# The start of a down-projection without a barrier, and its raw rows in seven slots

## The reference

```
g_pre, val = split(rmsnorm(x) @ w_ffn_up, 2)      # 1024 -> 2 x 2816
g          = causal_dwconv(g_pre, width 3)
x          = x + (gelu(g) * val) @ w_ffn_down     # 2816 -> 1024
y          = rmsnorm(x) * norm_final
```

## Time and profile before

| what | us |
|---|---|
| median of 3 runs | 3394.83 (3393.14 to 3395.13) |
| profiled execution, its own time | 3398.22 |
| its span | 3395.8 |
| first matmul of the down-projection at | 2817.30 |
| PE busy in the span | 3048.7 (90%) |
| ACT, DVE, POOL busy | 759.3, 1442.4, 1214.2 |

### The profile page before, as it was taken

The page is one execution under the profiler, slowest core; times in us unless marked ns, Lnnn a source line. Parts: engine busy times, 40 slices in busy tenths (PEclk is TensorE's granted clock), DMA queues, the critical chain, the costliest instruction groups (busy, mean ns, idle before and its releaser), DMA issues.

```text
span 3395.8 us, 47191 instructions
## 1 busy us (share of the span) xinstructions
PE 3048.7 (90%) x15400; PEld 2666.9 (79%) x15400; DVE 1442.4 (42%) x1910; ACT 759.3 (22%) x1530; POOL 1214.2 (36%) x574
## 2 busy tenths in 40 slices
PE   4898988956888888897899999999999997999998
PEld 4798978833444444446899999999999997899998
DVE  4212433348555555626215555544455542211221
ACT  5100332212232233334002000000000003443342
POOL 1011110144566666604765221222122213444443
PEclk8899999966899899998899999999999998999999
DMA  5311334355777776744344111111111104554553
GB/s 180 95 65 57 84 105 104 87 99 179 234 228 250 225 234 205 226 138 147 106 139 126 51 44 47 47 44 42 50 50 50 44 30 170 187 178 159 172 192 109
DMA packets 253579, 422.51 MB, mean 124 GB/s; under 512 B 49265, under 2 KB 156954, under 8 KB 248906
## 3 DMA queue, kind: packets, MB, share of 16 engines
q1 hardware_dynamic: 167986, 322.58, 30.5%
q10 hardware_dynamic: 85152, 97.07, 9.5%
q0 software_dynamic: 288, 1.05, 0.1%
HBM read 337.21 MB, written 83.46 MB: 124 GB/s over the span
## 4 chain that ended last, share of the span: by engine, by line
PE 67%; DMA 9%; POOL 8%; DVE 6%; issue 4%; SPq 3%; ACT 2%; POOLq 0%; ACTq 0%; DVEq 0%
PE PS L2413 33%; PE PS L2115 13%; PE PS L2499 4%; PE PS L2501 3%; PE PS L2500 3%; POOL prod L870 3%; DMA Kpg<-in_cache_k 3%; PE PS L2307 2%; DMA GR<-gT 2%; SPq L565 2%; PE PS L2404 1%; SPq L558 1%; POOL DL L990 1%; PE PS L2096 1%; DMA xin<-in_x_prompt 1%
## 5 line engine op out<-in xcount | busy, mean ns | idle before, releaser
L2413 PE MATMUL PS<-MH,VH 128*128 128x416 f32 x2000 | 708.3, 354 | 11.6 <-POOL VL L933 8.3
L2413 PE MATMUL PS<-ML,VH 128*128 128x416 f32 x2000 | 702.3, 351 | 0.0
L2413 PE MATMUL PS<-MH,VL 128*128 128x416 f32 x2000 | 701.9, 351 | 0.0
L2413 PEld LDWEIGHTS PS<-MH,VH 128*128 128x128 f32 x2000 | 376.1, 188 | 18.7 <-issue 13.3
L990 POOL TENSOR_TENSOR DL<-DR,DH 128x1408 fp32r<-128x1408 f32 x80 | 258.5, 3231 | 354.2 <-ACT DH L1410 354.0
L927 POOL TENSOR_TENSOR VR<-VR,gains 128x1024 f32<-128x1024 f32 x52 | 98.8, 1900 | 795.9 <-PE PS L2413 695.4
L2413 PEld LDWEIGHTS PS<-ML,VH 128*128 128x128 f32 x2000 | 377.2, 189 | 4.2 <-issue 0.8
L2413 PEld LDWEIGHTS PS<-MH,VL 128*128 128x128 f32 x2000 | 376.5, 188 | 4.8
L2499 PE MATMUL PS<-GH,DH 128*128 128x416 f32 x880 | 320.9, 365 | 46.7 <-POOL DL L990 28.3
L870 POOL TENSOR_TENSOR prod<-Kpg,qb 128x1024 f32<-128x1024 f32 x118 | 284.2, 2408 | 172.6 <-DMA Kpg<-in_cache_k 135.7
L2307 PE MATMUL PS<-PT,VA 128*65 128x416 f32 (+16 forms) x816 | 337.1, 498 | 4.5 <-ACT PT L1264 4.0
(11 more groups left out here) (274 smaller groups left out, 4604.9 us busy)
## 6 DMA issues: line engine op xcount, KB each, us to landing
Kpg<-in_cache_k SPq DMA_DIRECT2D x256, 256.0 KB, 4.3
Vpg<-in_cache_v SPq DMA_DIRECT2D x256, 256.0 KB, 4.2
DR<-in_w_down SPq DMA_DIRECT2D x80, 704.0 KB, 4.1
gT<-GO ACTq DMA_DIRECT2D x110, 208.0 KB, 1.9
GR<-gT SPq DMA_DIRECT2D x55, 416.0 KB, 4.9
VR<-in_w_up SPq DMA_DIRECT2D x44, 512.0 KB, 3.5
WR<-in_w_stream SPq DMA_DIRECT2D x21, 512.0 KB, 3.6
Qst<-qT SPq DMA_DIRECT2D x16, 520.0 KB
```

What stands on the lines that cost most here:

```text
L2413: mm = e.matmul(PS[:, j, 0:BW], w[:, u, k], x[:, k, cols(j)], start=(k == 0 and q == 0), stop=(k == KC - 1 and q == 2))
```

## The change

**The barrier goes.** Each engine has its own waits instead. The `m4` tiles are laid out so that some lie where the last up-chunk no longer reads: `GR` slots 0 to 2 and `DR[0]` over `VR` and the even weight slot of `VS` (which now holds `VH` and `VL`), free after chunk 50 (`u_mm >= 255`); `DH[0]` and `DL[0]` behind all the up-projection's tiles. `GH`, `GL`, the other four `GR` slots, `DR[1]` and the rest wait for the last up matmul (`u_mm >= 260`). `XS` moves to another stack.

**Work during the last up-chunk.** SP loads pairs 0 to 2 and `DR[0]`; POOL makes `DH[0]` (a copy of its own) and `DL[0]`.

**Seven raw slots** `GR` instead of three, so a `fetch_inner` waits for the pair seven before it. In block 0 it waits for the stores of its own rows too.

The core of the diff:

```diff
-            e.wait_ge(phase_end, 12)
+            e.wait_ge(v_lo, 52)
+            e.wait_ge(u_mm, 5 * 51)
...
             def fetch_inner(j, q):
                 f = FH * j + q
-                if f >= 3:
-                    e.wait_ge(gg_lo, f - 2)
-                e.dma_start(GR[:, f % 3], gT[...]).then_inc(gr_ld[f % 3], 16)
+                if j == 0:
+                    for st in go_st:
+                        e.wait_ge(st, 16 * NB * (q + 1) + 1)
+                if f >= NGR:
+                    e.wait_ge(gg_lo, f - NGR + 1)
+                e.dma_start(GR[f % NGR], gT[...]).then_inc(gr_ld[f % NGR], 16)
...
             fetch_down(0, 0, 0)
             for q in range(1, 3):
                 fetch_inner(0, q)
+            e.wait_ge(u_mm, 5 * 52)
+            fetch_inner(0, 3)
             fetch_down(1, 0, 1)
-            fetch_x2(0, 0, 0, 0)
-            e.dma_start(gfin[:], ...)
-            for q in range(3, FH):
+            for q in range(4, NGR):
                 fetch_inner(0, q)
...
+                if j == 0:
+                    fetch_down(2, 1, 0)
+                    fetch_inner(0, 7)
+                    fetch_x2(0, 0, 0, 0)
+                    fetch_inner(0, 8)
+                    fetch_down(3, 1, 1)
+                    for q in range(9, FH):
+                        fetch_inner(0, q)
+                    fetch_x2(1, 1, 0, 1)
+                    e.dma_start(gfin[:], ...)
...
# GpSimd
-            e.sem_inc(phase_end, 1)
-            e.wait_ge(phase_end, 12)
+            e.wait_ge(dr_ld[0], 16)
+            e.tensor_copy(DH[0][:], DR[:, 0]).then_inc(d_hi, 1)
+            low_down(0, 0)
+            low_down(1, 1)
...
# ScalarE
-            for s in go_st: ...
-            e.sem_inc(phase_end, 1)
-            e.wait_ge(phase_end, 12)
+            e.wait_ge(u_mm, 5 * 52)
...
-            split_down(0, 0)
             for q in range(3):
                 inner_high(0, q)
+            e.wait_ge(d_lo, 1)
             split_down(1, 1)
             for q in range(3, FH):
                 inner_high(0, q)
+                if q == 7:
+                    split_down(2, 0)
...
                 act_pair(0, first=True)
-                with e.Fori(1, 3) as i:
-                    act_pair(i)
-                act_pair(3, last=True)
+                act_pair(1)
+                act_pair(2, fills=FILLS[0])
+                act_pair(3, last=True, fills=FILLS[1])
# VectorE and TensorE: the barrier's two lines go; dve_pair as act_pair
```

More of the change, by code:

```diff
@@ L30 @@
 FH = FC // 2
+NGR = 7
 RING = 16
@@ L55, with inner_landed @@
 BIG = -1e30
+def inner_landed(f):
+    return 16 * (f // NGR) + 16 + (32 * 4 * NS if f % NGR >= 3 else 0)
 class Steps:
@@ L349, in build @@
         GL = sb("GL", [P, RING, 2, BW], F32R, m4)
[L350 to L353, removed]
         YX = sb("YX", [P, 2, BW], F32, m4)
-        YT = sb("YT", [P, 4, DM], F32, m4)
-        ysq = sb("ysq", [P, 4, P], F32, m4)
+        gfin = sb("gfin", [P, DM], F32, m4)
         yr = sb("yr", [P, 4], F32, m4)
         yq = sb("yq", [P, 4, KC], F32, m4)
-        gfin = sb("gfin", [P, DM], F32, m4)
+        ysq = sb("ysq", [P, 4, P], F32, m4)
+        GRb = sb("GRb", [P, NGR - 3, 2, BW], F32, m4)
+        under = sb("under", [P, 2 * KC * TP - 2 * RING * 2 * BW - 2 * BW - DM - 4 - 4 * KC - 4 * P - 2 * (NGR - 3) * BW],
+                   F32, m4)
+        GRa = sb("GRa", [P, 3, 2, BW], F32, m4)
+        DR = sb("DR", [P, 2, FH, P], F32, m4)
+        YT = sb("YT", [P, 4, DM], F32, m4)
+        DH1 = sb("DH1", [P, FH, P], F32R, m4)
+        DL1 = sb("DL1", [P, FH, P], F32R, m4)
+        over = sb("over", [P, 6 * KC * P + FC * 4 + FC * 2 * NS + TP + TP + 2 + TP + 2 + 4 * BW + 2 * P - 6 * BW - 2 * FH * P
+                           - 4 * DM - 2 * FH * P], F32, m4)
+        DH0 = sb("DH0", [P, FH, P], F32R, m4)
+        DL0 = sb("DL0", [P, FH, P], F32R, m4)
+        DH, DL = (DH0, DH1), (DL0, DL1)
+        GR = [GRa[:, n] for n in range(3)] + [GRb[:, n] for n in range(NGR - 3)]
         m4.close()
@@ L483, in build @@
         dk = sem("dk")
-        gr_ld = [sem(f"gr_ld{s}") for s in range(3)]
+        gr_ld = [sem(f"gr_ld{s}") for s in range(3)] + kg_ld
         gg_hi = sem("gg_hi")
@@ L766, in sync_pair @@
                             fetch_x2(8 * j + oc + 2, 0 if last else oc + 2, j + 1 if last else j, 0)
-                        if last and ahead:
+                        if j < NB - 1:
                             for q in fills[c]:
                                 fetch_inner(j + 1, q)
-                with e.Fori(0, 3) as i:
-                    sync_pair(i)
-                sync_pair(3, True)
+                if j == 0:
[7 more added lines that the diff above has]
+                    fetch_x2(1, 1, 0, 1)
+                    e.dma_start(gfin[:], a["norm_final"][0].partition_broadcast(P)).then_inc(nf_ld, 16)
+                    fetch_down(4, 2, 0)
+                    fetch_down(5, 2, 1)
+                    fetch_x2(2, 2, 0, 0)
+                    sync_pair(1)
+                else:
+                    with e.Fori(0, 2) as i:
+                        sync_pair(i)
+                sync_pair(2, False, FILLS[0])
+                sync_pair(3, True, FILLS[1])
         @block.gpsimd
@@ L982, in _, with low_down @@
             e.wait_ge(nlo, 15)
+            e.wait_ge(nst, 15)
+            e.wait_ge(nhi, 20)
             e.wait_ge(v_lo, 52)
-            e.sem_inc(phase_end, 1)
-            e.wait_ge(phase_end, 12)
-            with e.Fori(0, 8 * NB) as i:
+            def low_down(n, h):
+                e.wait_ge(d_hi, n + 1)
+                e.tensor_tensor(DL[h][:], DR[:, h], DH[h][:].bitcast(F32), ALU.subtract).then_inc(d_lo, 1)
+                e.wait_ge(d_lo, n + 1)
+            e.wait_ge(dr_ld[0], 16)
+            e.tensor_copy(DH[0][:], DR[:, 0]).then_inc(d_hi, 1)
+            low_down(0, 0)
+            low_down(1, 1)
+            with e.Fori(1, 8 * NB) as i:
                 for h in range(2):
-                    e.wait_ge(d_hi, 2 * i + h + 1)
-                    e.tensor_tensor(DL[:, h], DR[:, h], DH[:, h].bitcast(F32), ALU.subtract).then_inc(d_lo, 1)
-                    e.wait_ge(d_lo, 2 * i + h + 1)
+                    low_down(2 * i + h, h)
         @block.scalar
@@ L1456, in _, with act_pair @@
                 inner_high(0, q)
+                if q == 7:
+                    split_down(2, 0)
             for j in range(NB):
-                def act_pair(i, first=False, last=False):
+                def act_pair(i, first=False, last=False, fills=((), (), (), ())):
                     n, oc = 16 * j + 4 * i, 8 * j + 2 * i
-                    fills = {0: (0, 1, 2), 1: (3, 4), 2: (5, 6, 7, 8, 9), 3: (10,)}
                     for c in range(4):
-                        if not (j == NB - 1 and last and c == 3) and not (j == 0 and first and c == 0):
+                        if not (j == NB - 1 and last and c == 3) and not (j == 0 and first and c < 2):
                             split_down(n + c + 1, (c + 1) % 2)
@@ L1473, in act_pair @@
                             take_sum(oc, 2 * i, 0)
-                        if last and j < NB - 1:
+                        if j < NB - 1:
                             for q in fills[c]:
@@ L1485, in _ @@
             e.wait_ge(y_st, 64 * NB + 16)
+            for s in go_st:
+                e.wait_ge(s, 16 * NB * FC // 2 + 1)
+            for s in tt_st:
+                e.wait_ge(s, 16 * FC + 1)
+            e.wait_ge(f_st, 96)
         @block.vector
@@ L2061, in _, with dve_pair @@
                 inner_low(0, q)
-            e.wait_ge(nf_ld, 16)
             for j in range(NB):
-                def dve_pair(i, first=False, last=False):
+                def dve_pair(i, first=False, fills=((), (), (), ())):
                     oc = 8 * j + 2 * i
-                    fills = {0: (0, 1, 2), 1: (3, 4), 2: (5, 6, 7, 8, 9), 3: (10,)}
                     for c in range(4):
-                        if last and j < NB - 1:
+                        if j < NB - 1:
                             for q in fills[c]:
@@ L2078, in _ @@
                 dve_pair(0, first=True)
-                with e.Fori(1, 3) as i:
-                    dve_pair(i)
-                dve_pair(3, last=True)
+                dve_pair(1)
+                dve_pair(2, fills=FILLS[0])
+                dve_pair(3, fills=FILLS[1])
             final_apply(NB - 1)
```

41 lines of the change are left out of this document (14 added, 27 removed).

## The result

The changed kernel takes 3353.92 us in the median of 4 runs (3347.84 to 3359.2), the kernel before 3394.98 (3393.14 to 3402.36): a ratio of 0.9871, 95% interval 0.9854 to 0.9888. The profiled execution took 3355.78 us, its span 3353.6. The prediction was 3353.

A forecast was written before the change was run, and what follows sets the result against it. TensorE was taken to bound the kernel by standing still or running slowly at the barrier, the first rows and block ends; -10.3 + 0.5 - 6.7 - 25, taken as -42, gave 3353 us, range 3343 to 3371.

The forecast's parts named there:

- The first idle time: At the barrier before the down-projection: PE's idle time falls from 14.53 to 4.2 us, -10.3 us.
- POOL under the last up-chunk: Last up-chunk: POOL's copy and subtraction hold DVE up to 6.4 us; 0.5 us reaches the end, bounds 0 and 3.1.
- The first rows: First three halves of the down-projection: 26 us from PE's start against 32.7 before, -6.7 us.
- The 1 us for slow matmuls: First three halves: allowance for slow matmuls after idle times, 1.6 to 2.8 us each, part hidden under row waits.
- The block ends: Ends of blocks 0 to 3: of 28.1 us lost there 3 stay, -25 us.
- What stays: Each later block's first pair: a store wait holds ACT 3.41 us, untouched by the change; seven chunks take 92.2, not 90.1.
- The sum: Whole kernel: -10.3 + 0.5 - 6.7 - 25 = -41.5 us, taken as -42.
- Block ends giving half back: Ends of blocks: rows land later and stalls drag slow matmuls, 4 x 4 us more, -29, 3366 us; chance 0.20.
- waits only exchanged at the start: First three halves: third half ends as late after PE's start, POOL's `DL` blocking DVE's lows; near 3361 us; chance 0.09.
- Slower by row copies ahead of weight copies: Row copies ahead of weight copies in six halves a block, not four, make ACT late; 3402 us; chance 0.03.

The follow-up runs named there:

- the repetition: The changed kernel run once more, unaltered, on the chip of two other follow-up kernels: 3357.03 us, ratio 0.9858 to the kernel before.
- the swap: Changed kernel with y-store issues and first `take_sum` behind weight copies, new start order, and row loads ahead of `fetch_x2`: 3346.71 us, ratio 0.983.
- the spreading alone: Changed kernel with three raw row slots in place of seven, the spread placing of row loads kept: 3364.3 us, ratio 0.9904.

## Why the prediction was right, step by step

- **The first idle time.** Forecast 4.2 us, measured 4.25, ended by `GL` on DVE. The term of -10.3 is right for the kernel as it stands; the experiments divide X in other parts, since a barrier also delays what is issued behind it.
- **POOL under the last up-chunk.** Its copy took 1.36 us, bounded at 3.2, its subtraction 3.23. DVE's op beside the subtraction took 3.50 us, where the same line takes 0.65 elsewhere. In all DVE is busy for 18.03 us in the last up-chunk and was for 14.84: 3.2 us more, not 6.4. All of it is absorbed, since DVE waits as long for PE ahead of its last multiply as before, 3.30 us against 3.29. So 0 reached the end and not 0.5. The Trainium skill's rule (SBUF — State Buffer, Who interferes with whom) holds as to the blocking; the 3.1 us at the end that the prediction worked out with it did not appear. POOL, then DVE:

```profile
2787.61 1.36 POOL L1029 CAST DH<-DR 128x1408 fp32r<-128x1408 f32 x1 [22.14 <-DMA DR<-in_w_down]
2789.05 3.23 POOL L1025 TENSOR_TENSOR DL<-DR,DH 128x1408 fp32r<-128x1408 f32 x1
```

```profile
2789.23 3.50 DVE L2029 SCALAR_TENSOR_TENSOR GC<-GP,ftab,GC 128x416 f32<-128x416 f32 x1
...
2805.15 0.59 DVE L2052 TENSOR_TENSOR GO<-GC,R 128x416 f32<-128x416 f32 x1 [3.30 <-PE PS L2452]
```

- **The first rows.** 26 us forecast from PE's start to the third half's end, 25.3 measured in the first profile and 27.1 in the repetition. Both waits foreseen came, for pair 3 and pair 8, and they ended 6.7 and 15.5 us after PE's start, where 7.2 and 15.7 were forecast. The size of the first was not worked out right: by the prediction's own times PE would have waited 3.8 us for pair 3, not "about 2", and it waited 1.53, since slow matmuls had filled the time (5.2 us for three pairs instead of 3.4). The second came as 2.83, 2.9 by its times. The 1 us for slow matmuls was a guess between two outcomes, 0 and 1.6 us behind pair 8, and the two profiles show one each.
- **The block ends.** 3 us forecast to stay, 1.8 measured, where it was expected: at half 17, not at half 16. That the loads behind `fetch_x2` are the cause is shown by the swap, which takes it to 0 in its one profile. What the prediction gave to "seven slots" and to "three row copies instead of five" in one breath, the experiments separate: for the ends the spreading alone is enough.
- **What stays.** The chunk of 14.87 us stayed in all four blocks, but its cause was misread. I took a wait with a name for the cause and did not look at what stood ahead of the late weight copy in ACT's queue. It changed no term of the sum.
- **The sum.** -42 forecast; -42.2 between the two spans. That they agree to 0.2 us is in part luck: +2.2 come from the phases ahead of the change, -1.6 from one slow chunk before, and X moves by 1.8 from profile to profile.
- **Rivals.** Block ends giving half back, and waits only exchanged at the start: neither came. Slower by row copies ahead of weight copies: pair 2 shows no wait. The undisturbed chunks take 12.92 us, where before they were 12.84 and 12.92 by turns, about 1 us in all; its cause stays open.

## What to carry to other kernels

In hand-ordered queues a late instruction is late for what stands in front of it, so look at the queue up to it, not at the wait that the view names. Spreading prefetches until few stand ahead of an urgent copy can be worth as much as deeper buffers, and where it is, the buffers' gain lies elsewhere, here at the cold start. A barrier costs more than the idle time behind it: everything issued behind it is late too, and loads moved ahead of it recover only a part.

## What the runs showed of the hardware

- A DVE op with two SBUF operands begun during a GpSimd subtraction ended only behind it, by 0.4 to 0.9 us: 3.50 instead of 0.65 us, and 3.41 and 3.33 instead of 1.03.
- Behind one and the same wait (2.83 and 2.84 us) PE ran on at the higher level in one profile and fell to the lower for ten matmuls in another: 1.6 us. The estimate of this start cannot be closer than that.
- One program's phases ahead of the change moved by up to 17 us from profile to profile (2796.8 to 2813.8 for the same matmul), and on one chip by 16.6 (2797.0 and 2813.6). Differences under 0.3% were seen only by stages.
